# Two moves at the ends of the expert gathers: weight loads wait for the last gathered row, and the first rows' combinations go ahead of the fifth and sixth query

## The chip, the cores and the metric

One Trainium2 chip, one of its cores. The metric is the device time of one execution in microseconds (us), lower is better; of the kernel before three runs are given and their median counts. The engines are TensorE (PE), VectorE (DVE), ScalarE (ACT), GpSimd (POOL), and SyncE (SP), which only issues transfers.

## What is computed

Two transformer blocks over 256 tokens of width 1024, in float32. The stage at issue is the product-key expert layer of the first block: each of 8 heads of a token makes a query, scores it against two sets of 128 keys, takes the 16 best pairs, and mixes the 16 experts so found.

```
def peer(h, wq, subkeys, u, v):
    q = (ht @ wq).reshape(T, P_HEADS, 2, P_DKH)
    s = jnp.einsum('thcd,hcnd->thcn', q, subkeys).astype(jnp.float32)
    ...
    sc, ci = lax.top_k(cand, P_TOPK)
    e = jnp.take_along_axis(i1, ci // P_TOPK, axis=-1) * N_KEYS + jnp.take_along_axis(i2, ci % P_TOPK, axis=-1)
    g = jax.nn.softmax(sc, axis=-1)
    ...
        ub = jnp.take(u, eb, axis=0)
        z = jnp.einsum('thkd,td->thk', ub, hb)
        a = (jax.nn.gelu(z.astype(jnp.float32)) * gb).astype(hb.dtype)
        return jnp.einsum('thk,thkd->td', a, jnp.take(v, eb, axis=0))
```

The output of this layer is normed, added, and goes into the second block (attention, a linear recurrence, a squared-relu MLP), whose weights are streamed from HBM.

## The kernel before

The kernel is one hand-ordered program per engine, joined by semaphores. Tokens stand in two tiles `a` of 128. Weights come as loads of 1 MB (SP, L2239) into ring slots, two chunks to a load; of each chunk ScalarE writes a high part (`hi`, L976) and VectorE a low part (`lo`, L1429), and TensorE multiplies high and low parts separately. There are three buffers for the parts, so `hi` of chunk n waits until TensorE has used chunk n - 3. Chunks WQ0 to WQ0 + 15 are the query weights, called chunk 0 to 15 below; chunks 16 to 19 belong to the next block's q (`q2`), chunk 20 on to its k (`k2`).

**The gathers.** 256 "rows" i = 0 to 255 are fetched. A row is one indirect transfer by POOL (L2186): for each of the 128 tokens of a tile one expert's u and v, 8 KB, together 1 MB. Sixteen rows make one head of one tile (`ITS`). Row i goes to one of 11 slots (`ROW_SLOT`); slots 4 to 6 are ring slots, slots 7 to 10 are buffers in which query weights stood before. POOL issues in the order of i, and row i waits for the indices (`ei`: the first 8 of them come early, row 16 needs the second head's), for the combination of the row before in its slot (row 9 for row 0, row 14 for row 4, row 19 for row 8, row 23 for row 12), or, where a slot is used first, for the low parts of the chunks that stood there: row 7 for chunk 3's, row 8 for chunk 5's, row 13 for chunk 7's, row 18 for chunk 9's.

**What is done with a row.** VectorE takes the product with the token (`dot`, L1858). Every fourth row ScalarE applies gelu to four results (L1235), VectorE weights them (`weight`, L1869: weight g for rows 4g to 4g + 3), and ScalarE writes four diagonal matrices (`diagonal`, L1243). TensorE multiplies diagonal and v half of the row into PSUM (L771, four matmuls a row): the combination, which frees the slot (`s_comb`). A diagonal of row i needs the combination of row i - 4. From row 248 on each row has its own gelu and weight.

**What is laid between.** TensorE makes `query(g)` (L440, L441, L444; 24 matmuls, from chunk g) and `scores(h)` (L674, two queries in, for both tiles) behind rows given by `QUERY_AT` and `SCORE_AT`; ScalarE evicts them (L1228 and L1217) at its own places in the same order. VectorE lays steps of the routing (`route`, by `ROUTE_AT`: none for rows 0 to 3, two behind each of rows 4 to 9, then mostly one), low parts of chunks, and `tokens_done` (the second tile's tokens, needed from row 16) between the dots.

**The end of the stage.** SP issues loads in order. The two loads of `q2` (I_Q2, I_Q2 + 1) go out during the gathers. Loads I_Q2 + 2 to I_Q2 + 4 go to slots 4 to 6, each behind the last row of its slot (rows 245, 246, 247); behind them stand a 512 KB norm row (L2229) and load I_Q2 + 5, whose slot is free by then. Behind row 255's combination come two norms (`experts_norm(1)`, L1001 and others) and then the next block's q product, for which ScalarE makes chunks 19 to 21.

Of the kernel before, what the change touches and what calls it, by code (L numbers as in the profile page):

```python
# [130 lines left out]
def build_program(nc, A, out):  # L131
# [13 lines left out]
    WQ0 = chunk_at["wq", 0]  # L145
# [60 lines left out]
    ROUTE_AT = [0 if i < 4 else 2 if i < 10 else int(i < 22 or i % 16 >= 6 or i % 16 < 2) for i in range(226)] + [0] * 30  # L206
    EXP_AFTER = {2: 1, 4: 2} | {4 * n + 3: n + 2 for n in range(1, 14)}

    QUERY_AT = {3: (6, 7), 7: (8,), 11: (9,)} | {16 * n + 3: (8 + n,) for n in range(2, 6)} | {131: (14,), 147: (15,)}
    SCORE_AT = {16 * n + 7: (n + 3) // 2 for n in range(1, 10, 2)} | {16 * 10 + 7: 7}  # L210


# [5 lines left out]
    def landed(i):  # L218
        return s_gath[ROW_SLOT[i]], 16 * ROW_SLOT[:i + 1].count(ROW_SLOT[i])
# [10 lines left out]
    I_WQ, I_Q2 = load_at["wq", 0], load_at["q2", 0]  # L230
# [179 lines left out]
    def tensor_program(e):  # L410
# [3 lines left out]
        def bank(b):  # L414
            for s, v in frees[b]:
                e.wait_ge(s, v)
            return banks[b]
# [6 lines left out]
        def split_done(n):  # L424
            e.wait_ge(s_hi, n + 1)
            e.wait_ge(s_lov, n + 1)
            return chunk_of(n)[2:]
# [5 lines left out]
        def product(name, f, b, xh, xl_, by_k=None):  # L433
            n = chunk_at[name, f]
            hi, lo = high_done(n)
            pb = bank(b)
            for k in range(8):
                if by_k:
                    by_k(k)
                e.matmul(pb[:, 0:256], hi[:, k, :], xh[:, k, :], start=k == 0, stop=False)  # L440
                e.matmul(pb[:, 0:256], hi[:, k, :], xl_[:, k, :], start=False, stop=False)  # L441
            e.wait_ge(s_lov, n + 1)
            for k in range(8):
                r = e.matmul(pb[:, 0:256], lo[:, k, :], xh[:, k, :], start=False, stop=k == 7)  # L444
            r.then_inc(*o.inc(s_chunk, n + 1))
# [242 lines left out]
        def query(g):  # L688
            product("wq", g, g % 3, hfh, hfl)
            frees[g % 3] = ((s_q, g + 3),)  # L690
# [35 lines left out]
        for c in range(2):  # L726
            hi, lo = split_done(WQ0 + c)
# [23 lines left out]
        query(2)  # L751
        query(3)
        scores(1)
        query(4)
        query(5)
        acc = [[bank(4 + 2 * a + j) for j in range(2)] for a in range(2)]

        def block_features(a, two):
# [7 lines left out]
        for n, (a, h) in enumerate(ITS):  # L766
            for k in range(16):
                i = 16 * n + k
# [6 lines left out]
                r.then_inc(*o.inc(s_comb, i + 1))  # L775
                for g in QUERY_AT.get(i, ()):
                    query(g)
# [173 lines left out]
        for g in range(32):  # L951
            hi, lo = split_done(chunk_at["dn", g])
# [15 lines left out]
    def scalar_program(e):  # L968
        o = Own(s_act)

        def hi(n):
            i, v, h, _ = chunk_of(n)
            e.wait_ge(*arrived(i))
            if n >= NB:
                e.wait_ge(s_chunk, n - NB + 1)
            e.activation(h, v, AF.Copy).then_inc(*o.inc(s_hi, n + 1))  # L976
# [236 lines left out]
        def scores(h):  # L1213
            if h >= 2:
                e.wait_ge(s_ei, 2 * h - 2)
            e.wait_ge(s_score, SC_DONE[h, 1])
            e.activation(sct[:, h % 2, :, :], banks[3][:, :].rearrange("p (a b) -> p a b", a=4), AF.Copy).then_inc(  # L1217
                *o.inc(s_sct, SC_DONE[h, 1]))

        def query(g):  # L1220
            e.wait_ge(s_chunk, WQ0 + g + 1)
            if g // 2 in (5, 7):
                e.wait_ge(s_score, SC_DONE[{5: 0, 7: 5}[g // 2], 1])
            elif g // 2 == 6:
                e.wait_ge(s_h2s, 4)
            else:
                e.wait_ge(s_hu, 4)
            e.activation(qTs[g // 2][:, g % 2, :], banks[g % 3][:, 0:256], AF.Copy).then_inc(*o.inc(s_q, g + 3))  # L1228
# [42 lines left out]
        hi(WQ0 + 4)  # L1271
        query(2)
        hi(WQ0 + 5)
        query(3)
        hi(WQ0 + 6)
        scores(1)
        for n in range(16):
            if 1 <= n < 7:
                hi(WQ0 + 9 + n)
            elif 12 <= n < 15:  # L1280
                hi(WQ0 + 4 + n)
            for q in range(4):
                g = 4 * n + q
                if g == LAST // 4:
                    break
                gelu(g)
                for i in range(4 * g, 4 * g + 4):
                    diagonal(i)
                if g in EXP_AFTER:
                    route_exp(EXP_AFTER[g])  # L1290
                if g == 0:
                    for c in (4, 5):
                        query(c)
                        hi(WQ0 + c + 3)
                for c in QUERY_AT.get(4 * g + 3, ()):
                    query(c)
                    if c == 6:
                        hi(WQ0 + 9)
                if 4 * g + 3 in SCORE_AT:
                    scores(SCORE_AT[4 * g + 3])  # L1300
                if g in (56, 57):
                    load_sqrt()
                    experts_square(0) if g == 56 else block_square(0)
                    load_gelu()
                if g == 59:
                    for f in range(2):
                        features_hi(0, f, banks[f], "h3")
# [115 lines left out]
    def vector_program(e):  # L1423
        o = Own(s_vec)

        def lo(n):
            _, v, h, l = chunk_of(n)
            e.wait_ge(s_hi, n + 1)
            e.tensor_tensor(l, v, h.bitcast(f32), ALU.subtract).then_inc(*o.inc(s_lov, n + 1))  # L1429
# [153 lines left out]
        for g in range(8):  # L1583
            n = chunk_at["qk"[g // 4], g % 4]
# [343 lines left out]
        for i, _ in enumerate(route(0)):  # L1928
            if i == 1:
                tokens_scale(1)  # L1930
            if i == 9:
                for g in range(2):
                    features_lo(1, g, banks[(4, 5)[g]], "h2")
                lo(WQ0 + 2)
        lo(WQ0 + 3)
        tokens_done(0)
        norm0 = experts_norm(0)
        rt, n_rt = route(1), 1
        for i in range(256):
            dot(i)  # L1940
            for _ in range(ROUTE_AT[i]):
                if next(rt, rt) is rt and n_rt < 15:
                    n_rt += 1
                    rt = route(n_rt)
            if i in (1, 3, 4, 6, 8, 10):
                lo(WQ0 + {1: 4, 3: 5, 4: 6, 6: 7, 8: 8, 10: 9}[i])
            if i == 9:
                tokens_done(1)
            if i % 16 == 4 and 1 <= i // 16 < 7:
                lo(WQ0 + 9 + i // 16)  # L1950
            elif i % 16 == 4 and 12 <= i // 16 < 15:
                lo(WQ0 + 4 + i // 16)
            if i < LAST and i % 4 == 3:
                weight(i // 4)
            if i == 233:
                lru_rate()
            if i in NORM_AT:
                next(norm0, None)
            if i >= LAST:
                last_weight(i)  # L1960
# [241 lines left out]
    def sync_program(e):  # L2202
        last_chunk = {i: n for n, (_, i, _, _) in enumerate(chunks)}

        def released(i):
            name = loads[i][0]
            if name[0] == "adc":
                j = name[1]
                e.wait_ge(s_ada0, name[1] + 1)
            elif name[0] == "ada":  # L2210
                e.wait_ge(s_accR, 4 * name[1] + name[2] + 1)
            elif name[0] == "sk":
                e.wait_ge(s_tr, TR["sk", 3])
            else:
                e.wait_ge(s_lov, last_chunk[i] + 1)

        for r0, src in P0:
            e.dma_start(rows0[r0:r0 + src.shape[0], :], src).then_inc(s_p0, 16)
        for i in range(8):
            e.dma_start(places[i], A["weights"][i]).then_inc(s_ring[i], 16)  # L2220
            if i == 1:
                for a in range(2):
                    e.dma_start(xs[:, a, :], A["x"][0][128 * a:128 * a + 128, :]).then_inc(s_x, 16)
        for i in range(8, len(loads)):
            if i == I_WQ + 5:
                e.dma_start(g3[:, :], A["norm1_g_2"][0].partition_broadcast(128)).then_inc(s_n2, 16)
            if i == I_Q2 + 5:
                e.wait_ge(s_sct, SC_DONE[6, 1])
                e.dma_start(bcs[:, 1, :], A["norm2_g_2"][0].partition_broadcast(128)).then_inc(s_n2, 16)  # L2229
            if BEFORE[i] is not None:  # L2230
                released(BEFORE[i])
            else:

                e.wait_ge(s_mix, 8)
                e.wait_ge(s_adab, 8)
            if I_Q2 + 2 <= i < I_Q2 + 5:
                last = max(r for r in range(256) if ROW_SLOT[r] == 4 + UV_SLOTS.index(SLOT[i]))
                e.wait_ge(s_comb, last + 1)
            e.dma_start(places[SLOT[i]], A["weights"][i]).then_inc(s_ring[SLOT[i]], 16)  # L2239
        for a in range(2):  # L2240
            for c in range(2):
                e.wait_ge(s_xo, 2 * a + c + 1)
                e.dma_start(out[0][128 * a:128 * a + 128, 512 * c:512 * c + 512],
                            xs[:, a, 512 * c:512 * c + 512]).then_inc(s_out, 16)
        e.wait_ge(s_out, 64)
# [28 lines left out]
```

## Time and profile before

| | before |
|---|---|
| three runs | 1342.13, 1339.54, 1343.59 us |
| median | 1342.13 us |
| the profiled execution, own time | 1338.6 us |
| its span, first to last instruction | 1336.7 us |
| mean granted TensorE clock | 0.958 of 2.4 GHz |
| busy: TensorE, VectorE, ScalarE, GpSimd | 87%, 70%, 39%, 25% |
| first row issued, last row issued | 360.84, 1004.61 us |
| share of the end-chain in which a gather is waited for | 26% (21% gbuf, 5% ring) |

Times inside the profile are us from the span's start. The own time of the execution lies 1.9 us over its span and 3.5 us under the median. A wait is shown as idle time of an engine with what ended it ("<-"). The stage of the gathers reaches from 360 to about 1030 us.

### The profile page before, as it was taken

Reading aid. Unit: us, or ns where it says so; the run is one execution under the profiler, and the core shown is the slowest. Engines: PE = TensorE matmul, PEld = TensorE weight load, DVE = VectorE, ACT = ScalarE, POOL = GpSimd, SP = SyncE. Lnnn points to the kernel's source line nnn. Section 1 sums busy time; section 2 is a strip of 40 time slices with the busy share of each in tenths; the row PEclk is TensorE's granted clock in tenths of the full one; section 3 lists DMA queues with packets and bytes.
Section 4 is the critical chain, followed back from the end, with each engine's and each line's share of the span. In section 5 each row is a group of like instructions: output and inputs, shape, how many; then the busy total and the mean of one; then the engine's idle time right before and its main releaser. Section 6 shows DMA issues by size and latency. Waiting matters only on the chain.

```text
span 1336.7 us, 15753 instructions
## 1 busy us (share of the span) xinstructions
PE 1168.0 (87%) x5582; PEld 819.0 (61%) x5582; DVE 931.3 (70%) x1894; ACT 517.4 (39%) x988; POOL 327.6 (25%) x310
## 2 busy tenths in 40 slices
PE   5889999999898878888787888877888999999999
PEld 5878989998774334434333333333333797899787
DVE  6974788787777877677776677777754686666544
ACT  4555434454542312223212222212522477555432
POOL 4000000000134544444445444544540100000000
PEclk8899999999899999989889999889988999999999
DMA  8763367686489999999999999999996431454550
GB/s 363 290 246 129 110 240 274 241 332 235 152 363 340 420 428 426 426 427 427 427 427 427 427 427 427 427 427 427 427 427 272 152 140 63 160 188 167 210 186 36
DMA packets 57697, 405.68 MB, mean 303 GB/s; under 512 B 6908, under 2 KB 7108, under 8 KB 9108
## 3 DMA queue, kind: packets, MB, share of 16 engines
q0 software_dynamic: 38576, 272.49, 48.9%
q1 hardware_dynamic: 19044, 132.19, 26.6%
q8 instruction: 45, 0.74, 0.2%
q14 instruction: 32, 0.26, 0.0%
HBM read 403.61 MB, written 1.05 MB: 303 GB/s over the span
## 4 chain that ended last, share of the span: by engine, by line
PE 41%; DMA 27%; DVE 18%; ACT 8%; issue 6%; POOL 0%; SPq 0%; DVEq 0%; ACTq 0%; POOLq 0%
DMA gbuf<-in_peer_uv,ei 21%; PE bank L771 11%; DMA ring<-in_peer_uv,ei 5%; DVE wlo L1429 5%; PE bank L444 4%; PE bank L440 4%; PE bank L441 4%; ACT whi L976 4%; DVE gbuf L1858 3%; PE bank L962 2%; PE bank L961 2%; PE bank L960 2%; PE bank L455 1%; PE bank L461 1%; PE bank L456 1%
## 5 line engine op out<-in xcount | busy, mean ns | idle before, releaser
L771 PE MATMUL bank<-gbuf,dg 128*128 128x512 f32 x748 | 364.9, 640 | 88.8 <-ACT dg L1243 88.8
L1429 DVE TENSOR_TENSOR wlo<-ring,whi 128x1024 fp32r<-128x1024 f32 x188 | 228.4, 1223 | 151.3 <-ACT whi L976 151.2
L771 PEld LDWEIGHTS bank<-gbuf,dg 128*128 128x128 f32 x748 | 148.6, 204 | 294.7 <-issue 172.9
L1858 DVE CUSTOM_DVE_ANT_0 gbuf<-gbuf,h2t 128x1024 f32<-128x1024 f32 x187 | 228.7, 1224 | 106.8 <-DMA gbuf<-in_peer_uv,ei 105.6
L2186 POOL DMA_INDIRECT gbuf<-in_peer_uv,ei x187 | 220.2, 1177 | 334.4 <-PE bank L771 200.9
L976 ACT ACTIVATE whi<-ring 128x1024 fp32r<-128x1024 f32 x188 | 196.4, 1051 | 90.0 <-PE bank L962 47.7
L771 PE MATMUL bank<-ring,dg 128*128 128x512 f32 x276 | 134.3, 632 | 29.1 <-ACT dg L1243 28.7
L1235 ACT ACTIVATE za<-za 128x4 f32<-128x4 f32 x62 | 12.6, 204 | 290.9 <-DVE za L1858 290.8
L440 PE MATMUL bank<-hh,whi 128*128 128x256 f32 x448 | 113.7, 292 | 6.5 <-ACT hh L1048 3.2
L771 PEld LDWEIGHTS bank<-ring,dg 128*128 128x128 f32 x276 | 54.0, 201 | 102.9 <-issue 64.0
L440 PE MATMUL bank<-hfh,whi 128*128 128x256 f32 x432 | 112.1, 297 | 4.8 <-issue 4.3
L1858 DVE CUSTOM_DVE_ANT_0 ring<-ring,h2t 128x1024 f32<-128x1024 f32 x69 | 84.2, 1222 | 39.2 <-DMA ring<-in_peer_uv,ei 38.8
L441 PE MATMUL bank<-hl,whi 128*128 128x256 f32 x448 | 110.3, 284 | 0.0
L2186 POOL DMA_INDIRECT ring<-in_peer_uv,ei x69 | 84.1, 1219 | 90.8 <-PE bank L771 69.1
L441 PE MATMUL bank<-hfl,whi 128*128 128x256 f32 x432 | 106.3, 284 | 0.0
L1243 ACT ACTIVATE dg<-ident,za 128x128 f32<-128x128 f32 x256 | 82.7, 391 | 30.5 <-DVE za L1869 27.9
L440 PEld LDWEIGHTS bank<-hh,whi 128*128 128x128 f32 x448 | 86.1, 192 | 8.9 <-issue 5.7
L440 PEld LDWEIGHTS bank<-hfh,whi 128*128 128x128 f32 x432 | 82.8, 192 | 8.7 <-issue 7.3
L441 PEld LDWEIGHTS bank<-hl,whi 128*128 128x128 f32 x448 | 86.3, 193 | 0.5 <-issue 0.5
L441 PEld LDWEIGHTS bank<-hfl,whi 128*128 128x128 f32 x432 | 83.0, 192 | 2.2 <-issue 2.2
L444 PE MATMUL bank<-hh,wlo 128*128 128x256 f32 x448 | 62.7, 282 | 0.4 <-DVE wlo L1429 0.4
L444 PE MATMUL bank<-hfh,wlo 128*128 128x256 f32 x432 | 60.5, 283 | 0.0
(395 smaller groups left out, 1724.0 us busy)
## 6 DMA issues: line engine op xcount, KB each, us to landing
ring<-in_weights SPq DMA_DIRECT2D x116, 1024.0 KB, 4.9
gbuf<-in_weights SPq DMA_DIRECT2D x4, 1024.0 KB, 10.0
gbuf<-in_peer_uv,ei POOLq DMA_INDIRECT x187, 14.7
bcs<-in_b_ada POOLq DMA_DIRECT2D x3, 512.0 KB, 11.0
ring<-in_peer_uv,ei POOLq DMA_INDIRECT x69
xs<-in_x SPq DMA_DIRECT2D x2, 512.0 KB, 8.1
ya<-in_weights SPq DMA_DIRECT2D x1, 1024.0 KB, 17.2
qkT<-in_weights SPq DMA_DIRECT2D x1, 1024.0 KB, 19.0
```

The costliest lines, as they stand in the source:

```text
L440: e.matmul(pb[:, 0:256], hi[:, k, :], xh[:, k, :], start=k == 0, stop=False)
L441: e.matmul(pb[:, 0:256], hi[:, k, :], xl_[:, k, :], start=False, stop=False)
L444: r = e.matmul(pb[:, 0:256], lo[:, k, :], xh[:, k, :], start=False, stop=k == 7)
L771: r = e.matmul(acc[a][j][:, :], dg[:, i % 4, :], expert_rows(i)[:, 1024 + 512 * j:1536 + 512 * j], start=h == 0 and k == 0, stop=h == 7 an ...
L960: e.matmul(q, l_h, hi[:, 0, s_], start=g == 0, stop=False)
L961: e.matmul(q, l_h, lo[:, 0, s_], start=False, stop=False)
L962: r = e.matmul(q, l_l, hi[:, 0, s_], start=False, stop=g == 31)
L976: e.activation(h, v, AF.Copy).then_inc(*o.inc(s_hi, n + 1))
L1243: e.activation(dg[:, i % 4, :], ident[:, :], AF.Copy, scale=za[:, i // 16 % 2, 16 + i % 16:17 + i % 16]).then_inc(*o.inc(s_dg, i + 1))
L1429: e.tensor_tensor(l, v, h.bitcast(f32), ALU.subtract).then_inc(*o.inc(s_lov, n + 1))
L1858: e.tensor_tensor_reduce(row, row, h2t[:, ITS[n][0], :], 1.0, 0.0, ALU.mult, ALU.add, za[:, n % 2, i % 16:i % 16 + 1]).then_inc(*o.inc(s_d ...
L2186: e.indirect_dma_start(out=expert_rows(i), out_offset=None, in_=A["peer_uv"], in_offset=bass.IndirectOffsetOnAxis(ap=ei[:, a, at:at + 1], ...
```

## The change

Three things are done. SP's load I_Q2 + 2 waits, beside what it waited for, until row 255 has landed. TensorE makes queries 4 and 5 behind row 3 and no longer ahead of row 0; queries 6, 7, 8 and 9 go from behind rows 3, 3, 7 and 11 to behind rows 7, 11, 15 and 19. ScalarE has query 3, chunk 6 and scores 1 behind rows 0 to 3's diagonals, and all later query and score evictions one group of four rows later; VectorE's low parts of chunks 3, 7, 8 and 9 go behind rows 0, 8, 9 and 13 (from ahead of row 0, and behind rows 6, 8 and 10), and `tokens_done(1)` from behind row 9 to behind row 12.

```
-    QUERY_AT = {3: (6, 7), 7: (8,), 11: (9,)} | {16 * n + 3: (8 + n,) for n in range(2, 6)} | {131: (14,), 147: (15,)}
+    QUERY_AT = {3: (4, 5), 7: (6,), 11: (7,), 15: (8,), 19: (9,)} | {16 * n + 3: (8 + n,) for n in range(2, 6)} | {131: (14,), 147: (15,)}
...
         scores(1)
-        query(4)
-        query(5)
         acc = [[bank(4 + 2 * a + j) for j in range(2)] for a in range(2)]
...
         hi(WQ0 + 5)
-        query(3)
-        hi(WQ0 + 6)
-        scores(1)
+
+        def queries(i):
+
+            for c in QUERY_AT.get(i, ()):
+                query(c)
+                if 4 <= c < 7:
+                    hi(WQ0 + c + 3)
+            if i in SCORE_AT:
+                scores(SCORE_AT[i])
+
...
                 if g == 0:
-                    for c in (4, 5):
-                        query(c)
-                        hi(WQ0 + c + 3)
-                for c in QUERY_AT.get(4 * g + 3, ()):
-                    query(c)
-                    if c == 6:
-                        hi(WQ0 + 9)
-                if 4 * g + 3 in SCORE_AT:
-                    scores(SCORE_AT[4 * g + 3])
+                    query(3)
+                    hi(WQ0 + 6)
+                    scores(1)
+                else:
+                    queries(4 * g - 1)
...
-        lo(WQ0 + 3)
         tokens_done(0)
...
-            if i in (1, 3, 4, 6, 8, 10):
-                lo(WQ0 + {1: 4, 3: 5, 4: 6, 6: 7, 8: 8, 10: 9}[i])
-            if i == 9:
+            if i in (0, 1, 3, 4, 8, 9, 13):
+                lo(WQ0 + {0: 3, 1: 4, 3: 5, 4: 6, 8: 7, 9: 8, 13: 9}[i])
+            if i == 12:
                 tokens_done(1)
...
+            if i == I_Q2 + 2:
+                e.wait_ge(*landed(255))
             if I_Q2 + 2 <= i < I_Q2 + 5:
```

ScalarE at the first rows. Here `bc` and `bcs` take queries, `sct` scores, `whi` a chunk's high part, `za` the four gelu results and `dg` a diagonal. Before:

```order
L976 ACTIVATE whi<-gbuf 128x1024 [waits s_chunk,s_early4]
L1228 ACTIVATE bc<-bank 128x256 [waits s_h_gained,s_chunk]
L976 ACTIVATE whi<-gbuf 128x1024 [waits s_chunk,s_early5]
L1217 ACTIVATE sct<-bank 128x512 [waits s_score_mm]
L1235 ACT_TABLE_LOAD
L1235 ACTIVATE za<-za 128x4 [waits s_dot]
L1243 ACTIVATE dg<-ident,za 128x128 [waits s_wgt]
L1243 ACTIVATE dg<-ident,za 128x128 x3
L1228 ACTIVATE bc<-bank 128x256 [waits s_h_gained,s_chunk]
```

and changed:

```order
L974 ACTIVATE whi<-gbuf 128x1024 [waits s_chunk,s_early4]
L1233 ACT_TABLE_LOAD
L1233 ACTIVATE za<-za 128x4 [waits s_dot]
L1241 ACTIVATE dg<-ident,za 128x128 [waits s_wgt]
L1241 ACTIVATE dg<-ident,za 128x128 x3
L1226 ACTIVATE bc<-bank 128x256 [waits s_h_gained,s_chunk]
L974 ACTIVATE whi<-gbuf 128x1024 [waits s_chunk,s_early5]
L1215 ACTIVATE sct<-bank 128x512 [waits s_score_mm]
L1233 ACTIVATE za<-za 128x4 [waits s_dot]
```

The first gelu and the first four diagonals stand ahead of query 3, chunk 6 and scores 1, and no further query stands ahead of the second gelu.

SP at the end of the gathers, where `s_combine` counts combinations and `s_gather9` counts what landed in row 255's slot. Before:

```order
L2239 DMA ring<-in_weights 128x2048 [waits s_lo_vec] x5
L2239 DMA ring<-in_weights 128x2048 [waits s_combine,s_lo_vec] x2
L2239 DMA ring<-in_weights 128x2048 [waits s_combine,s_transposed]
L2229 DMA bcs<-in_norm_g 128x1024 [waits s_sct]
```

and changed:

```order
L2241 DMA ring<-in_weights 128x2048 [waits s_lo_vec] x5
L2241 DMA ring<-in_weights 128x2048 [waits s_combine,s_gather9,s_lo_vec]
L2241 DMA ring<-in_weights 128x2048 [waits s_combine,s_lo_vec]
L2241 DMA ring<-in_weights 128x2048 [waits s_combine,s_transposed]
L2229 DMA bcs<-in_norm_g 128x1024 [waits s_sct]
```

Only the first of the three loads has the new wait; the order of issue is as before.

## Rows read from the trace of the kernel before

**Rows 1.** Stretches: length, busy time of PE, PEld, DVE, ACT, POOL; PE clock, DMA share, GB/s.

```profile
380.00:440.00 60.00, 53.06 (x224) 32.58 (x224) 47.42 (x127) 21.11 (x45) 23.19 (x22) 0.97 0.88 340
440.00:1000.00 560.00, 456.62 (x1106) 204.02 (x1104) 403.08 (x999) 143.94 (x372) 267.70 (x225) 0.94 1.01 427
...
1022.00:1030.00 8.00, 5.67 (x8) 1.63 (x6) 2.90 (x6) 1.21 (x4) 0.00 (x0) 0.57 0.24 100
...
1040.00:1100.00 60.00, 59.23 (x352) 51.66 (x353) 45.46 (x70) 35.55 (x47) 3.63 (x6) 1.00 0.46 163
```

**Rows 2.** Timeline of POOL: start, duration; issues of rows 9, 13, 14, 18, 23.

```profile
388.21 0.94 POOL L2186 DMA_INDIRECT gbuf<-in_peer_uv,ei  x1 [8.03 <-PE bank L771]
...
395.56 0.94 POOL L2186 DMA_INDIRECT gbuf<-in_peer_uv,ei  x1 [0.30 <-issue]
402.23 1.30 POOL L2186 DMA_INDIRECT ring<-in_peer_uv,ei  x1 [5.73 <-PE bank L771]
...
410.29 1.18 POOL L2186 DMA_INDIRECT gbuf<-in_peer_uv,ei  x1 [1.97 <-DVE wlo L1429]
...
428.70 0.94 POOL L2186 DMA_INDIRECT gbuf<-in_peer_uv,ei  x1 [6.54 <-PE bank L771]
```

**Rows 3.** Timeline of PE: scores 1, combinations of rows 0 to 3, of 248 to 251.

```profile
378.95 1.13 PE L674 MATMUL bank<-skT,bc 128*128 128x128 f32 x8 [0.56 <-ACT bc L1228]
...
385.55 7.03 PE L771 MATMUL bank<-gbuf,dg 128*128 128x512 f32 x16
...
1008.82 7.03 PE L771 MATMUL bank<-gbuf,dg 128*128 128x512 f32 x16
```

**Rows 4.** Timeline of ACT: chunk 5's high part, first gelu's table, diagonals 0 to 3, query 6.

```profile
375.82 1.05 ACT L976 ACTIVATE whi<-gbuf 128x1024 fp32r<-128x1024 f32 x1
...
380.74 1.28 ACT L1235 ACT_TABLE_LOAD   x1
...
382.60 1.28 ACT L1243 ACTIVATE dg<-ident,za 128x128 f32<-128x128 f32 x4 [0.36 <-DVE za L1869]
...
395.43 0.39 ACT L1228 ACTIVATE bcs<-bank 128x256 f32<-128x256 f32 x1 [8.35 <-PE bank L444]
```

**Rows 5.** Timeline of DVE: weight 0, dot 5, weight 1, chunk 9's low part.

```profile
382.34 0.22 DVE L1869 SCALAR_TENSOR_TENSOR za<-za,rx 128x4 f32<-128x4 f32 x1 [3.80 <-ACT za L1235]
...
386.52 1.22 DVE L1858 CUSTOM_DVE_ANT_0 ring<-ring,h2t 128x1024 f32<-128x1024 f32 x1
...
398.75 0.22 DVE L1869 SCALAR_TENSOR_TENSOR za<-za,rx 128x4 f32<-128x4 f32 x1 [2.70 <-ACT za L1235]
...
408.30 1.22 DVE L1429 TENSOR_TENSOR wlo<-gbuf,whi 128x1024 fp32r<-128x1024 f32 x1
```

**Rows 6.** DMA view of 360 to 450 us: GB/s in 40 slices of 2.25 us.

```profile
GB/s 0 244 422 419 411 411 444 419 419 437 415 160 11 204 422 426 422 430 422 76 364 382 422 419 426 306 331 269 411 441 320 211 313 335 411 426 430 419 419 430
```

**Rows 7.** Timeline of DVE at the end: dots of rows 251, 252, 255.

```profile
1009.36 1.23 DVE L1858 CUSTOM_DVE_ANT_0 gbuf<-gbuf,h2t 128x1024 f32<-128x1024 f32 x1 [0.70 <-DMA gbuf<-in_peer_uv,ei]
...
1014.27 1.23 DVE L1858 CUSTOM_DVE_ANT_0 gbuf<-gbuf,h2t 128x1024 f32<-128x1024 f32 x1 [3.18 <-DMA gbuf<-in_peer_uv,ei]
...
1027.84 1.22 DVE L1858 CUSTOM_DVE_ANT_0 gbuf<-gbuf,h2t 128x1024 f32<-128x1024 f32 x1 [1.98 <-DMA gbuf<-in_peer_uv,ei]
```

**Rows 8.** Timeline of SP's queue, 1000 to 1062 us: first and last start, count.

```profile
1005.63 3.76 SPq L2239 DMA_DIRECT2D ring<-in_weights  x3
...
1009.91 49.29 SPq L2239 DMA_DIRECT2D ring<-in_weights  x5
```

**Rows 9.** Chain that ended last: the flights of row 247 (in ring) and row 255.

```profile
984.50 15.11 DMA ring<-in_peer_uv,ei
...
1004.61 23.21 DMA gbuf<-in_peer_uv,ei
```

**Rows 10.** Page, DMA issues: count, size, median us to landing.

```profile
ring<-in_weights SPq DMA_DIRECT2D x116, 1024.0 KB, 4.9
```

**Rows 11.** Timeline of ACT: chunk 20's high part, the first of `k2`.

```profile
1043.91 1.06 ACT L976 ACTIVATE whi<-ring 128x1024 fp32r<-128x1024 f32 x1 [0.34 <-PE bank L801]
```

## The prediction

> **What bounds the kernel now.** I read first the table of stretches. From 440 to 1000 us the DMA engines are busy all the time and move 427 GB/s, while TensorE is busy 456.62 of 560 us and VectorE 403.08 [rows 1]. A gathered row is 128 x 8 KB, 1.0486 MB, so at 427 GB/s a row costs 2.456 us; the row combination is not what the time goes by, the transfers are. So in this stage only two things can save time: DMA time that goes unused, and bytes that need not be moved ahead of the last row. Both exist. From 380 to 440 us only 340 GB/s were moved [rows 1]: (427 - 340) / 427 x 60 = 12.2 us of transfer time unused. And at the end of the stage the products of rows (the dots) start 2.4 us apart until 1009.36 and then at 1014.27 and so on, the last at 1027.84, waiting for DMA each time [rows 7].
>
> Next the POOL queue, for what holds the early issues. Rows 0 to 8 have a free buffer; row 9 waits until row 0 is combined (issued 388.21), row 14 for row 4 (402.23), row 18 for the low part of chunk 9 (410.29), row 23 for row 12 (428.70) [rows 2]. TensorE makes row 0 to 3's combinations from 385.55 in 7.03 us, 1.72 us a row; between the scores that end at 379.9 and them stand queries 4 and 5, 5.7 us [rows 3]. ScalarE stood idle for 8.35 us in front of a query eviction whose products TensorE had not made yet, and only behind it and one more came the gelu of the next four rows [rows 4]; VectorE waited 3.80 us for the first gelu and 2.70 for the second [rows 5]. So queries on ScalarE hold the first rows' weights.
>
> **The change, part by part: the start.** The instructions are the same in number; they move.
>
> ScalarE reaches the first gelu without query 3, its chunk, and scores 1. Before, those ended at about 380.7, the table load took 1.28 and weight 0 ran at 382.34 [rows 4, 5]. Now what stands ahead of the gelu is chunk 5's high part, ended at 376.9 [rows 4]; 376.9 + 1.28 + 0.20 + 0.2 gives weight 0 at 378.6, 3.7 us earlier. The price: scores 1 on TensorE stands ahead of row 0's combination and needs query 3's eviction, now behind four diagonals (1.28 us [rows 4]): 378.8 + 1.28 + 0.38 = 380.5. Scores take 1.1, so combination 0 starts at 381.6, not 385.55: 4 us, not the 5.7 us of two queries. Combinations 0 to 3 end at 383.5, 385.2, 386.9, 388.6; with 0.7 us to the issue, row 9 is issued at 384.1 (was 388.21) and row 12 at 389.3.
>
> TensorE then makes queries 4 and 5 until 394.3. On VectorE 4.18 us lie between weight 0 and dot 5 [rows 5]: 0.14 the weight, 1.14 a dot, 1.13 a low part, which leaves 0.9 for each of two routing steps. Weight 1 was at 398.75 [rows 5]. Off this come 3.8 for the earlier start, 2.7 of waiting, and 1.1 for chunk 7's low part, now behind row 8: 391.2. Rows 4 to 7's diagonals are there at 392.8, so combinations 4 to 7 run right behind query 5, 394.3 to 401.4. The moved low part of chunk 7 has a cost: row 13's buffer waits for it. ScalarE makes its high part behind query 4, at 393.2 to 394.2, the low part ends at 395.4, and row 13 goes at 396.1, against 395.56 before [rows 2]: nothing gained. Rows 14 to 17 follow at 397.8, 399.5, 401.2, 402.9; row 16 also needs the next 16 indices, written behind dot 9 at 397.6.
>
> Row 18 waits for chunk 9's low part, now behind dot 13, not dot 10. From 391.2: the 10.7 us that lay between weight 1 at 398.75 and that low part's end at 409.4 [rows 5], plus chunk 7's low part 1.1, three dots 3.4, and three routing steps with weight 2, 2.6 us: about 409. Row 18 at 409.9, was 410.29: again nothing gained. But behind it rows 19 to 22 need combinations 8 to 11, which now run 404.2 to 411.2 (query 6 ahead), and row 23 needs row 12's, ready at about 416, so it goes at 418.4 instead of 428.70 [rows 2].
>
> The sum of the start goes by DMA time. Transfers begin some 2.2 us behind an issue: row 9 was issued at 388.21, and the slice from 387.0 to 389.25 moved 11 GB/s, the next 204 [rows 6]. The first row was issued at 360.84, so nine rows of 2.456 keep the engines from 363 until 385: idle until 386.3 = 1.3; row 12 ends at 396.1, row 13 starts at 398.3 = 2.2; row 17 ends at 410.7, row 18 starts at 412.1 = 1.4; behind it always a row is queued. That leaves 5 of 12.2 us unused: **7.2 us gained**. Bounds: if every moved step comes 3 us later than I have it and the pieces at row 13 and 18 grow by that, about 1; if only 2 us stay idle, 10.
>
> **The change, part by part: the end.** The three loads of slots 4 to 6 are issued from 1005.63, behind them the 512 KB norm row and one more load at 1009.91 [rows 8]: 4.5 MB, ahead of rows that were already queued. Row 255, issued at 1004.61, took 23.21 us to land, where an undisturbed row took 15.11 [rows 9]: 8.1. By the spacing, row 251's dot starts at 1009.36 and four rows of 2.456 would put row 255's at 1019.2, not 1027.84 [rows 7]: 8.7. I take 8.4. All five transfers stand behind the one wait, since SP issues in order. The skill's page "DMA: Bandwidth & Descriptors" (Queues, rings and completion order) says that a DMA engine turns between its queues packet by packet; with equal shares all 4.5 MB would pass ahead of row 255, an estimate of 11 us for this term instead of 8.4. The trace agrees in kind: dots 4.91 us apart are two transfers a row [rows 7]. Bounds: 6 (if only the three loads' excess goes and a latency comes back) to 11.
>
> What is late next: those loads are now issued at about 1019.5. The median load of the kernel lands in 4.9 us [rows 10], so the first is there at 1024.4 and the last (4.5 MB, 10.8 us) at about 1032.5. The first user is ScalarE's high part of chunk 20, at 1043.91 [rows 11], then at 1035.3: 10.9 us to spare. The second load's user comes 8 us behind. So they cost nothing. TensorE keeps up with rows 2.46 us apart, at 1.72 us a row; the combinations of rows 248 to 251 already end at 1015.85 in the trace [rows 3], so row 255's is done some 2 us behind its dot, within ScalarE's table load as now.
>
> **Sum.** 7.2 + 8.4 = 15.6 us off the profiled execution's 1338.6 gives 1323.0. That execution lay 3.5 under the median of the runs, 1342.13; against the median the forecast is **1326.5**. The stages behind the gathers are TensorE-bound (59.23 of 60 us busy from 1040, DMA 0.46 [rows 1]) and only start earlier.
>
> **The rivals.** A: the start gives nothing, only the end. For it: rows 13 and 18, tied to ScalarE's chunk copies behind queries, are issued no earlier in my own walk; if the chain comes 3 us later, the engines idle there instead. Against: rows 14 to 17 and 19 to 23 do come 4 to 10 us earlier. It gives 1342.1 - 8.4 - 1 = 1332.7.
>
> B: the end gives nothing; the wait moves. The bytes are the same and the first k2 load would hold ScalarE. For it: the skill's same page (Issuing engines are not separate DMA queues) has transfers of all queues on the same 16 engines, so reordering saves no transfer time. Worked out from rows, it needs the first load 10.9 us later than I have it; against it stands that the DMA share is 0.24 from 1022 to 1030 and 0.46 from 1040 [rows 1]: there is room. It gives 1342.1 - 7.2 = 1334.9.
>
> C: neither, or the moved steps cancel: 1340 to 1344.
>
> D, slower: the circle row 13, chunk 7, dot 8, gelu 1, diagonals, query 4, and then row 18, chunk 9, dot 13, becomes the bound. VectorE would wait for a row that is issued only behind a low part which stands behind an earlier row. Its place is the issue of row 18. Each us of delay there, past 409.9, is a us idle; the end's 8.4 and the start's 7.2 are used up when row 18 goes at 425.5, and slower by over 0.3% (4 us, about what a measurement can tell from no change) begins at 429.5. With row 18 at 431 the time would be 1348. Against: dot 13 needs only row 13, issued 396.1, some 10 us ahead.
>
> **How the numbers follow.** Forecast (both parts, at least half of the start) 0.72; A 0.15; B 0.06; C 0.04; D 0.03. The range takes both terms' bounds: 3 + 6 us of gain at the small end reaches 1333, A's 1332.7 is inside, and with the spread of runs I end at 1334; 10 + 11 is 1321. Faster by over 0.3% is forecast, A and B: 0.93; within 0.3% 0.04; slower 0.03.
>
> **What would show it.** Right: SP's ring loads issued behind the last dot's landing (near 1012, all of it shifted); last dots about 2.45 us apart to the end; row 255 landing in 15 us; row 9 issued near 384 and row 23 near 418; 380 to 440 at 385 GB/s or more; no ScalarE wait of 8 us for a query; weight 0 near 378.6. Wrong: a wait of ScalarE for the k2 load, GB/s of 380 to 440 near 340, or row 18 issued far behind 410.

## The result and the profile after

The changed kernel takes 1325.18 us (median of four runs, 1324.12 to 1326.00), the kernel before 1342.14 (1339.54 to 1343.59): ratio 0.9875, 95% interval 0.9858 to 0.9893, 17.0 us less. The profiled execution of the changed kernel took 1326.0 us, span 1324.0. In a second comparison it took 1324.74 against 1341.88. Of the nine executions of the kernel `act_only` below, two took 1615.89 and 5309.15 us, in the slow state, and are left out of its median.

The prefix up to the first gather is untouched but lasts differently from execution to execution: row 0 was issued at 360.84 us before and at 363.14 after, and at 362.64 in the trace of `wait_only` below, which has the start of the kernel before. The two profiled executions are only 12.6 us apart (1338.6 and 1326.0) because of these 2.3 us. So times of the start are told below from row 0's issue. From there to row 255's dot it was 667.0 us before (1027.84 - 360.84) and is 652.0 now: 15.0 us less, where the forecast's sum was 15.6. From row 255's dot to the end both traces have 308.9 us, so all of the change lies in the gathers.

Stretch of 60 us from 19.16 us behind row 0's issue, the same place as the first row of [rows 1], in the trace after (columns as there; the second row is the stretch that answers to 1022 to 1030):

```profile
382.30:442.30 60.00, 59.49 (x246) 36.17 (x247) 53.81 (x145) 21.25 (x47) 30.90 (x25) 0.97 0.96 383
...
1022.00:1030.00 8.00, 5.50 (x31) 4.41 (x30) 3.65 (x8) 2.98 (x8) 1.66 (x3) 1.00 0.82 316
```

383 GB/s and not 340: (427 - 383) / 427 x 60 = 6.2 us unused, where it was 12.2. TensorE is busy 59.49 of 60 us, where it was 53.06. Behind the last row the engines now carry the loads that went ahead of it: a share of 0.82 where it was 0.24.

The issues of rows 9, 13, 14, 18 and 23 on POOL after, which answer to [rows 2]:

```profile
387.86 1.92 POOL L2186 DMA_INDIRECT gbuf<-in_peer_uv,ei  x1 [4.83 <-PE bank L769]
...
398.73 1.17 POOL L2186 DMA_INDIRECT gbuf<-in_peer_uv,ei  x1 [4.47 <-DVE wlo L1430]
400.63 1.42 POOL L2186 DMA_INDIRECT ring<-in_peer_uv,ei  x1 [0.73 <-DVE ei L1832]
...
412.26 1.17 POOL L2186 DMA_INDIRECT gbuf<-in_peer_uv,ei  x1 [5.02 <-DVE wlo L1430]
...
421.89 0.94 POOL L2186 DMA_INDIRECT gbuf<-in_peer_uv,ei  x1 [0.30 <-issue]
```

Rows 13 and 18 wait for VectorE's low parts (`wlo`), as forecast, and row 23 for nothing. ScalarE, which stood 8.35 us for a query [rows 4], now stands for VectorE's dots:

```profile
380.56 0.21 ACT L1233 ACTIVATE za<-za 128x4 f32<-128x4 f32 x1
...
391.87 0.20 ACT L1233 ACTIVATE za<-za 128x4 f32<-128x4 f32 x1 [7.30 <-DVE za L1859]
...
395.36 0.38 ACT L1226 ACTIVATE bc<-bank 128x256 f32<-128x256 f32 x1 [0.47 <-PE bank L444]
```

The last dots on VectorE, rows 252 and 255, the chain's flight of row 255, and SP's queue at the end (answering to [rows 7], [rows 9] and [rows 8]):

```profile
1007.85 1.23 DVE L1859 CUSTOM_DVE_ANT_0 gbuf<-gbuf,h2t 128x1024 f32<-128x1024 f32 x1 [0.70 <-DMA gbuf<-in_peer_uv,ei]
...
1015.14 1.23 DVE L1859 CUSTOM_DVE_ANT_0 gbuf<-gbuf,h2t 128x1024 f32<-128x1024 f32 x1 [0.72 <-DMA gbuf<-in_peer_uv,ei]
```

```profile
1000.65 14.47 DMA gbuf<-in_peer_uv,ei
```

```profile
1015.17 1.28 SPq L2241 DMA_DIRECT2D ring<-in_weights  x3
1016.50 0.64 SPq L2229 DMA_DIRECT2D bcs<-in_norm_g  x1
1017.20 40.51 SPq L2241 DMA_DIRECT2D ring<-in_weights  x7
```

Rows now arrive 2.43 us apart to the last, row 255 lands in 14.47 and not 23.21 us (8.7 us less), and the loads go out as it lands. The other 6.3 us of the 15.0 lie ahead of row 255's issue (643.8 us behind row 0's before, 637.5 now).

### The profile page after: what moved, and what is told of

It reads as the page before. It is cut to its first block, busy times and chain, and to the rows that moved or that the text cites. A ratio compares the mean times of both kernels' runs of the same rounds, so it can differ in the third digit from the quotient of the medians.

```text
span 1324.0 us, 15753 instructions
## 1 busy us (share of the span) xinstructions
PE 1161.4 (88%) x5582; PEld 819.1 (62%) x5582; DVE 933.4 (70%) x1894; ACT 517.3 (39%) x988; POOL 338.8 (26%) x310
## 4 chain that ended last, share of the span: by engine, by line
PE 35%; DMA 33%; DVE 17%; ACT 8%; issue 6%; SPq 0%; POOL 0%; DVEq 0%; POOLq 0%; ACTq 0%
DMA gbuf<-in_peer_uv,ei 24%; DMA ring<-in_peer_uv,ei 8%; PE bank L769 6%; DVE wlo L1430 5%; ACT whi L974 4%; PE bank L444 4%; PE bank L440 4%; PE bank L441 4%; DVE gbuf L1859 3%; PE bank L958 2%; PE bank L960 2%; PE bank L959 2%; PE bank L455 1%; PE bank L456 1%; PE bank L461 1%
## 5 line engine op out<-in xcount | busy, mean ns | idle before, releaser
L769 PE MATMUL bank<-gbuf,dg 128*128 128x512 f32 x748 | 355.0, 626 | 78.8 <-ACT dg L1241 78.8
L769 PEld LDWEIGHTS bank<-gbuf,dg 128*128 128x128 f32 x748 | 145.3, 199 | 276.6 <-issue 168.4
L2186 POOL DMA_INDIRECT gbuf<-in_peer_uv,ei x187 | 230.0, 1230 | 315.4 <-PE bank L769 171.1
L769 PE MATMUL bank<-ring,dg 128*128 128x512 f32 x276 | 135.2, 636 | 32.6 <-ACT dg L1241 32.6
## 6 DMA issues: line engine op xcount, KB each, us to landing
gbuf<-in_peer_uv,ei POOLq DMA_INDIRECT x187, 14.7
```

The source lines that it names most:

```text
L769: r = e.matmul(acc[a][j][:, :], dg[:, i % 4, :], expert_rows(i)[:, 1024 + 512 * j:1536 + 512 * j], start=h == 0 and k == 0, stop=h == 7 an ...
L2186: e.indirect_dma_start(out=expert_rows(i), out_offset=None, in_=A["peer_uv"], in_offset=bass.IndirectOffsetOnAxis(ap=ei[:, a, at:at + 1], ...
```

## The experiments

Every kernel is told against the kernel before, timed on the same chip in the same hours (medians 1341.4 to 1342.0). The table puts their starts together: issue of a row in us behind row 0's issue, and GB/s in the 60 us from 19.16 us behind it. One trace stands for each kernel; how far such numbers vary between executions is seen from the two traces with the start of the kernel before and the five with the start of the change (the change, its repetition, `start_only`, `three_ahead`, `late_wait`).

| kernel | row 9 | row 13 | row 14 | row 18 | row 23 | GB/s |
|---|---|---|---|---|---|---|
| before | 27.4 | 34.7 | 41.4 | 49.5 | 67.9 | 340 |
| wait_only, the same start | 27.0 | 34.3 | 41.0 | 49.1 | 69.5 | 327 |
| the change | 24.7 | 35.6 | 37.5 | 49.1 | 58.8 | 383 |
| five traces with its start | 23.9 to 24.7 | 34.5 to 35.6 | 36.4 to 37.5 | 48.0 to 49.1 | 56.6 to 58.8 | 382 to 394 |
| pe_only | 25.0 | 36.8 | 45.9 | 53.9 | 72.7 | 310 |
| act_only | 29.9 | 38.0 | 42.4 | 52.8 | 61.8 | 361 |
| scores_behind | 20.8 | 35.0 | 36.5 | 48.6 | 57.8 | 391 |
| chunk9_first | 20.8 | 35.0 | 36.5 | 46.1 | 55.6 | 403 |
| chunk7_first | 21.1 | 32.6 | 35.2 | 46.4 | 55.9 | 411 |

### The wait alone

```
+            if i == I_Q2 + 2:
+                e.wait_ge(*landed(255))
             if I_Q2 + 2 <= i < I_Q2 + 5:
```

> The kernel before with the wait on the last gathered row alone. Theory (the 4.5 MB issued at 1005 us stood ahead of the last rows): 8.4 to 8.7 us faster than before, the last eight dots 2.44 us apart, row 255 landing in about 15 us. Rival (the wait only moves to the k2 load, same bytes): 0 to 2 us faster, and ScalarE waits for a load at chunk 20.

Measured: 1333.14 us against 1341.94, ratio 0.9933 (0.9921 to 0.9946), 8.8 us less. In its trace the dots of rows 251 to 255 take 9.73 us, where they took 18.48 [rows 7]: 8.7 us less. ScalarE does not wait for a load at chunk 20. The rival falls.

### The start alone

The change without these two lines.

> The change without the wait on the last row. Theory: the unused transfer time at the start falls by 6 to 7 us and all of it reaches the end: 6 to 8 us faster than before, last dots again 4.9 us apart. Rival (the start gives nothing, the end gave all): within 2 us of before. If the two parts are independent, this gain and that of the wait alone add up to the 17.0 us between the medians.

Measured: 1333.83 us, ratio 0.9941 (0.9928 to 0.9953), 8.1 us less. 8.8 and 8.1 make 16.9, and the whole change gave 17.0: the two parts add up. That fits the transfers' full rate between them (426 or 427 GB/s from 79 to 630 us behind row 0's issue in every trace), so that rows which start earlier also end earlier.

### Three loads ahead, the rest behind

```
             if i == I_Q2 + 5:
+                e.wait_ge(*landed(255))
...
-            if i == I_Q2 + 2:
-                e.wait_ge(*landed(255))
```

> The change, but the wait on the last row stands at the norm row and load I_Q2 + 5; the three loads of slots 4 to 6 go out after rows 245 to 247 as before. Theory (every MB issued ahead of the last row delays it by its transfer time, 2.46 us): 3 MB cost 7.4 us, so 1332.6 us, and the norm row and load 5 account only for the last 1.3 us of the 8.7. Rival (equal turns between two queues, so the share counts and not the bytes, and the norm row and load 5 cost their 3.7 us): some 5 us, 1330.

Measured: 1333.57 us (1330.88 to 1335.54), ratio 0.9936 (0.9923 to 0.9950); 8.4 us over the change's first median, 8.8 over its second. The medians alone do not tell 7.4 us from the 8.7 of all five transfers (each ratio is known to about 0.0015, 2 us). The trace gives the price more closely. Dots of rows 251 to 255 on VectorE:

```profile
1004.08 1.23 DVE L1859 CUSTOM_DVE_ANT_0 gbuf<-gbuf,h2t 128x1024 f32<-128x1024 f32 x1 [0.70 <-DMA gbuf<-in_peer_uv,ei]
1007.44 1.23 DVE L1859 CUSTOM_DVE_ANT_0 gbuf<-gbuf,h2t 128x1024 f32<-128x1024 f32 x1 [1.64 <-DMA gbuf<-in_peer_uv,ei]
1012.36 1.23 DVE L1859 CUSTOM_DVE_ANT_0 gbuf<-gbuf,h2t 128x1024 f32<-128x1024 f32 x1 [3.20 <-DMA gbuf<-in_peer_uv,ei]
1017.29 1.23 DVE L1859 CUSTOM_DVE_ANT_0 gbuf<-gbuf,h2t 128x1024 f32<-128x1024 f32 x1 [3.20 <-DMA gbuf<-in_peer_uv,ei]
1021.27 1.22 DVE L1859 CUSTOM_DVE_ANT_0 gbuf<-gbuf,h2t 128x1024 f32<-128x1024 f32 x1 [2.26 <-DMA gbuf<-in_peer_uv,ei]
```

Four rows take 17.19 us and not 4 x 2.44 = 9.76: 7.4 us, three loads of 2.46 in full. The kernel before lost 8.7 there, so the norm row and load 5, 1.5 MB behind the three, cost 1.3: most of them no longer got ahead of row 255.

### The loads later still

```
-                e.wait_ge(*landed(255))
+                e.wait_ge(s_fhi, FHI["h3", 3])
```

> The change, with the load I_Q2 + 2 held back about 12 us more, until the last tokens' high features are written (1027.2 us in the trace of the change) instead of row 255's landing (1015). Theory (10.9 us to spare at chunk 20): the load lands 4.9 us later at 1032.1, its user stood at 1031.2, so 0.5 to 2 us slower than the change, with ScalarE waiting for the ring load. Rival (the loads are hidden by far more): no change. Rival (each load behind it is late too, since they follow 2.46 us apart): 4 us or more slower.

Measured: 1324.55 us (ratio 0.9869, 0.9854 to 0.9884), the change's time. ScalarE does wait for the load, as the theory said:

```profile
1027.05 1.28 SPq L2241 DMA_DIRECT2D ring<-in_weights  x3
```

```profile
1031.83 2.01 ACT L974 ACTIVATE whi<-ring 128x1024 fp32r<-128x1024 f32 x2 [1.18 <-DMA ring<-in_weights]
```

but TensorE takes up chunk 20 only at 1034.93 and has work of chunk 19 until then:

```profile
1034.70 0.39 PE L799 MATMUL bank<-whi,hfl 128*128 128x512 f32 x1
1034.93 0.39 PE L455 MATMUL bank<-whi,hfh 128*128 128x512 f32 x1
```

So the loads could be more than the forecast's 10.9 us late without cost: the first user's own work was early too.

### TensorE's order alone

```
-    QUERY_AT = {3: (6, 7), 7: (8,), 11: (9,)} | ...
+    QUERY_AT = {3: (4, 5, 6, 7), 7: (8,), 11: (9,)} | ...
...
-        query(4)
-        query(5)
```

ScalarE keeps its old places for the evictions.

> Before, with TensorE's order alone changed: queries 4 and 5 behind row 3, ScalarE and VectorE as before. Theory (ScalarE's queries ahead of the second gelu set the issue of rows 14 on): row 9 is issued some 3 us earlier, rows 14 and on as before, so 0 to 2 us faster. Rival (the title's theory: TensorE's combinations behind two queries are what held the rows back, 5.7 us): 5 to 6 us faster.

Measured: 1345.90 us, ratio 1.0032 (1.0021 to 1.0042): 4.0 us slower. Neither theory said so. Row 9 is 2.4 us earlier (25.0), but row 14 is 4.5 us later (45.9) than before. ScalarE shows it; the eviction of query 4, the first of four ahead of the second gelu, and that gelu:

```profile
395.30 0.38 ACT L1227 ACTIVATE bc<-bank 128x256 f32<-128x256 f32 x1 [10.92 <-PE bank L445]
...
404.03 0.20 ACT L1234 ACTIVATE za<-za 128x4 f32<-128x4 f32 x1
```

Queries 4 to 7 stood ahead of the second gelu, and their products now come behind four combinations. The second gelu is 42.2 us behind row 0's issue and not 37.7 (398.52 in the kernel before). Part of these 4.5 us is TensorE's clock. In this order TensorE waits 3.06 us for the first diagonals, its granted clock is 0.50 from 385.9 to 387.9 us (its lower level, 1.2 GHz), and the four combinations take 8.80 us and not 7.03 [rows 3]:

```profile
383.65 8.80 PE L770 MATMUL bank<-gbuf,dg 128*128 128x512 f32 x16 [3.06 <-ACT dg L1242]
```

Without those 1.8 us the gelu would still come 2.7 us late, by the order alone (an estimate from these rows).

### ScalarE's and VectorE's order alone

The change of both, with TensorE's `QUERY_AT` and `query(4)`, `query(5)` as before, and no wait on the last row.

> The change of ScalarE's and VectorE's order alone, TensorE makes its queries as before, no wait on the last row. Theory (ScalarE's order counts most): 3 to 5 us faster than before; row 9 issued as before near 388, row 14 near 401. Rival (TensorE's order counts most): within 1 us of before or slower, since TensorE now waits for evictions that stand later.

Measured: 1337.71 us (the median of seven), ratio 0.9968 (0.9958 to 0.9979), 4.2 us less. The size is the theory's, its rows are not: row 9 goes at 29.9, 2.5 us later than before. TensorE's scores 1 wait 2.13 us for query 3's eviction and begin 1.0 us later; the granted clock is then 0.50 from 381.7 to 384.7 us, and the combinations, which still stand behind queries 4 and 5, begin another 1.5 us later. Row 14 is no earlier (42.4). Nearly all the gain is at row 23 and on (61.8 against 67.9), where the queries that held ScalarE are gone: the third gelu runs 44.3 us behind row 0's issue and not 49.9. A loss of 4.0 and a gain of 4.2 us alone, but a gain of 8.1 together: the two orders have to move as one.

### What is left at the start

Three steps, each on top of the one before, beginning with the change:

```
scores_behind: scores(1) on TensorE behind row 3; on ScalarE behind the second group's diagonals
chunk9_first:  query(6) and hi(WQ0 + 9) ahead of route_exp(1); lo(WQ0 + 9) at row 12, tokens_done(1) at row 13
chunk7_first:  scores(1), query(4), hi(WQ0 + 7) ahead of gelu(1); lo(WQ0 + 7) at row 7
```

> The change, with scores 1 behind row 3 on TensorE and behind the second group's diagonals on ScalarE. Theory (row 0's combination waits 2.1 us for scores that wait for query 3's eviction): row 9 is issued 2 us earlier, the hole in the transfers at 387 to 391 shrinks, 1 to 2 us faster than the change. Rival (rows 13 and 18 set the pace, so time won at row 9 is lost at row 13): 0.

> The kernel scores_behind, and besides query 6 with chunk 9's high part ahead of the second head's exponential on ScalarE, chunk 9's low part behind row 12 and tokens_done behind row 13. Theory: row 18 is issued 1.5 to 2 us earlier and the hole before it (about 1.4 us) closes: 1 to 1.5 us faster than scores_behind, 2 to 3.5 faster than the change. Rival: row 18's hole is covered by queued rows, 0.

> The kernel chunk9_first, and besides scores 1, query 4 and chunk 7's high part ahead of the second gelu on ScalarE (it idles 7 us there), chunk 7's low part behind row 7. Theory (row 13 waits for chunk 7's low part, and the hole of some 5 us in the transfers stands in front of it): row 13 is issued 2.6 us earlier, weight 1 up to 1.3 us later; 1 to 2.5 us faster than chunk9_first, about 1321. Rival (the later weight 1 takes it back): 0.

Measured: 1323.69, 1322.69 and 1322.12 us; ratios 0.9869 (0.9854 to 0.9884), 0.9852 (0.9837 to 0.9867) and 0.9848 (0.9832 to 0.9863). By the medians each step gives about 1 us, but the steps lie within each other's intervals, and scores_behind has the ratio of the change in its second comparison (0.9869). The traces tell more. From row 0's issue to row 255's dot it is 652.0, 652.4 and 652.5 us in three traces of the change's start with late loads, and 651.6, 649.9 and 648.6 us with the three steps. With scores behind, row 9 goes 3.9 us earlier (3.1 to 3.9 against the five traces), more than the 2 expected, but row 13 stands where those five have it: the hole in the transfers moves from in front of row 9 to in front of row 13, and the step is worth next to nothing by itself, as the rival said. Chunk 9 first brings row 18 2.5 us forward, chunk 7 first row 13 by 2.4, both more than the traces vary. The unused time, 6.2 us in the change (4.6 to 6.3 in the five traces), is 5.1, 3.4 and 2.2 with the steps (391, 403, 411 GB/s). Some 3 us of it show in the time: 2.6 by the medians of the same chip, 3.4 in the traces.

Why row 9 gains more than the 2 us of the wait: in the changed kernel TensorE waits 2.09 us for the eviction, and the four combinations behind take 8.73 us, not 7.03 [rows 3]:

```profile
382.81 1.13 PE L674 MATMUL bank<-skT,bc 128*128 128x128 f32 x8 [2.09 <-ACT bc L1226]
383.77 8.73 PE L769 MATMUL bank<-gbuf,dg 128*128 128x512 f32 x16
```

The stretch from 384 to 388 us has a granted clock of 0.57, that is TensorE's lower level, 1.2 GHz, for most of it:

```profile
384.00:388.00 4.00, 4.00 (x6) 1.54 (x5) 3.90 (x13) 0.57 (x1) 0.14 (x1) 0.57 0.97 389
```

All five traces with this start show it: a wait of 2.06 to 2.12 us, then combinations of 8.46 to 8.73 us. In scores_behind TensorE waits 0.98 us, the clock stays at 1.00 and the combinations take 7.11; they begin 2.6 us earlier and lose 1.6 us less.

### One MB more out of the gathers

On top of chunk7_first, the wait on the last row moves to q2's second load:

```
-            if i == I_Q2 + 2:
+            if i == I_Q2 + 1:
                 e.wait_ge(*landed(255))
...
-        q2_half(0, 0, 3)
+        q2_half(0, 0, 2)
         block_features(1, (2, 3))
+        cs_.append(split_done(chunk_at["q2", 2]))
+        q2_half(0, 2, 3)
```

and chunk 18 is split between the norms behind row 255 (ScalarE ahead of the last features, VectorE behind the diagonal).

> The kernel chunk7_first, with the wait on the last row put on load I_Q2 + 1 (q2's second MB), its first chunk split in the norms' idle times and multiplied behind the last tokens' transposes. Theory (each MB that leaves the gathers gives 2.46 us, and after row 255 the engines have room): 2 to 2.5 us faster than chunk7_first. Rival (the chain of norms behind row 255 has no room for one more chunk on three engines): 0 or slower.

Measured: 1320.71 us, ratio 0.9840 (0.9826 to 0.9855), 1.4 us under chunk7_first by medians, less than this pair of runs can tell for sure. In the traces row 255's dot is 2.4 us earlier behind row 0 (646.2 against 648.6), as one load's transfer gives. But from that dot to chunk 19's high part it is 16.2 us, not 14.7. TensorE had 2.41 us without work, and the transposes for the last tokens, 2.02 us in chunk7_first, took 3.58 at a granted clock of 0.59:

```profile
1016.00:1019.00 3.00, 0.59 (x4) 0.18 (x2) 2.70 (x7) 2.50 (x6) 0.00 (x0) 0.97 1.01 426
1019.00:1023.00 4.00, 4.00 (x19) 3.91 (x20) 1.92 (x2) 1.11 (x3) 0.00 (x0) 0.59 1.03 391
```

Last, the hole filled with nine matmuls whose result is overwritten:

```
         q2_half(0, 0, 2)
+        pb = bank(2)
+        for _ in range(9):
+            e.matmul(pb[:, :], hfh[:, 0, 0:128], cs_[0][0][:, 0, :], start=True, stop=True)
```

> The kernel q2_late with nine more matmuls of chunk 16 into a bank that is overwritten, between the first two chunks' products and the last tokens' transposes (their results are not used). In q2_late TensorE is idle for 2.4 us there, its granted clock falls to 0.59 and the 16 transposes take 3.58 us instead of 2.02. Theory (the clock took back 1.5 of the 2.4 us): the transposes take 2.0 us again and the time falls by 1 to 1.5 us, to about 1319.4. Rival (the clock does not matter there, the chain of three engines has its own length): 0.

Measured: 1320.67 us, ratio 0.9846 (0.9833 to 0.9859): no difference. Its trace:

```profile
1016.77 2.26 PE L809 MATMUL bank<-whi,hfh 128*128 128x512 f32 x9
1019.15 2.02 PE L485 MATMUL bank<-masks,h2t 128*128 128x128 f32 x16
```

The transposes take 2.02 us again, so the clock was their cost. But they begin 10.3 us behind row 255's dot (1008.81) and not 9.4, and of 1.56 us 0.6 are left (dot to chunk 19: 15.6 us). The nine matmuls are not what made them late: they end at 1019.03, and the diagonal that the transposes need is itself begun 9.9 us behind the dot (1018.72), not 9.0. The 0.9 us are older. ScalarE's first square behind row 255 has to wait for the last combination, because TensorE was still making up for a slow stretch at the combinations of rows 244 to 247:

```profile
991.56 2.39 PE L768 MATMUL bank<-gbuf,dg 128*128 128x512 f32 x4 [3.63 <-ACT dg L1247]
993.75 6.64 PE L768 MATMUL bank<-ring,dg 128*128 128x512 f32 x12
```

The granted clock was 0.50 from 994 to 996 us there; in q2_late, at the same place, the clock was 1.00 and the twelve matmuls took 5.31. So the medians compare executions in which the lower clock fell on different places, and what the nine matmuls are worth by themselves stays open.

The fastest versions, at 1320.7, beat the kernel before by 21 us and the change by 4.

## Why the prediction was right

**The end.** Forecast 8.4 us, between 8.1 by the flight and 8.7 by the spacing [rows 7, 9]. Measured 8.7 in the traces and 8.8 by the medians of the wait alone. The spacing was the better row: it compares with rows landing 2.44 us apart at the same moment, while row 247's flight of 15.11 us holds its own place in the queue. While both queues had work the dots stood 4.92 us apart, two transfers' time, so the two moved equal shares; but that all 4.5 MB would pass ahead of row 255, the estimate of 11 us, was too much: three loads cost 7.4 and the 1.5 MB behind them 1.3.

**The loads' cover.** Forecast 10.9 us to spare; no wait of ScalarE for a load shows, and 12 us more of delay cost nothing. Rival B is gone.

**The start.** Forecast 7.2 us; 6.3 in the two traces, 8.1 by the medians of the start alone. Executions vary by as much: row 251's dot stands 648.5 and 650.7 us behind row 0's issue in the two traces with the old start, 641.2 to 642.7 us in the five with the new. The walk holds place by place. Behind row 0's issue it had rows 9, 13, 14, 18, 23 at 23.3, 35.3, 37.0, 49.1, 57.6; measured 24.7, 35.6, 37.5, 49.1, 58.8. The one step clearly off is row 9, by 1.4 us: scores 1 and the first combination began when forecast (19.7 and 20.6 us behind row 0's issue), but I had the combinations at 1.72 us a row, which is the higher clock's price, and the combinations ran at the lower one. The start of the transfers was mis-sized too: bytes moved 1.6 us behind row 9's issue in the kernel before, where POOL's instruction lasted 0.94 us, and 2.5 us behind it after, where it lasted 1.92, and not 2.2. Read in slices of 2 us, some 3 us are unused at row 9, where the forecast had 1.3, 1.3 at row 13 (2.2) and 0.7 at row 18 (1.4). So 6.2 us stayed unused where the forecast had 5, and the sum came that near partly because an error at row 9 and two smaller ones behind it had opposite signs.

**The range.** Its small end takes 3 us for the start, where the forecast's own bound for it was about 1; with 1 and 6 us it would have been 1335. The result does not hang on it.

**Rival A** rested on rows 13 and 18 gaining nothing. They gained nothing clear (34.5 to 35.6 us for 34.7, 48.0 to 49.1 for 49.5), and still the part gave its time, because the rows between and behind them did; but the same two rows are what the later steps had to move. **Rival D** did not come up; row 18 went at 49.1 and the point of no gain was 64.7.

**What the title suggests** is less than what works. Combinations ahead of queries 4 and 5 on TensorE, alone, cost 4.0 us. The forecast's reading, that queries on ScalarE hold the weights, holds for the rows from 23 on, but ScalarE's and VectorE's order alone gave 4.2 of 8.1.

**Median and execution.** The forecast kept the profiled execution 3.5 us under the median. Much of that was the prefix: row 0's issue varied between 360.84 and 363.50 us in the traces, and that of the kernel before is the earliest of all. The changed kernel's profiled execution lay 0.8 us over its median, and 3.0 us over the 1323.0 forecast for it, 2.3 of them ahead of row 0's issue.

## What to carry to other kernels

In a stretch bound by transfers, count the bytes that go ahead of the last one that is waited for: each MB of a later stage that gets ahead of it costs its full transfer time (2.46 us here), and costs nothing behind the last row, as long as there is slack up to its first user, which a deliberately late wait measures. When work is moved on one engine of a chain, move its consumer's place on the other engines too, and walk the whole circle; a half of this change was slower than none. Where a removed hole brings less than its length, look for the next row whose buffer hangs on another engine: the hole has moved there.

## What the runs showed of the hardware

Several waits of TensorE of 2 to 3 us were followed by a granted clock near 0.5 for some 3 us, its lower level of 1.2 GHz. At the start it was so in all seven traces in which such a wait stood there (2.06 to 2.13 us, and 3.06 in pe_only), and the four combinations behind took 8.46 to 8.80 us instead of 7.03 where they came next. Behind row 255 it was a wait of 2.41 us, and the transposes took 3.58 us instead of 2.02. With the slower work behind it a wait cost 1.6 to 1.8 times its length at these places. Behind waits of 0.94 to 1.00 us at the same two places it did not happen.

The length of the wait does not decide it. Of 28 waits of 2 to 3 us of TensorE between 440 and 1000 us in the trace of the change, 11 were followed by a clock of 0.57 to 0.63 over the next 4 us and 17 by 1.00. One of each, waits of 2.56 and 2.40 us:

```profile
506.17:510.17 4.00, 4.00 (x6) 1.82 (x7) 3.61 (x5) 0.82 (x3) 0.20 (x1) 0.60 1.03 428
535.72:539.72 4.00, 4.00 (x10) 1.85 (x11) 3.31 (x7) 3.95 (x8) 1.24 (x1) 1.00 1.01 426
```

What sets the two kinds apart is not shown here. In the stretch of the gathers it cost no time, since the transfers kept their 427 GB/s; it counts where TensorE's work is what the next row or the next stage waits for.
